# A two-block transformer layer on one core: the residual adds and a LayerNorm's gain moved from GpSimd to VectorE

## What is computed

```python
def rmsnorm(x, g):
    return x * rsqrt(mean(x * x) + EPS) * g
def layer_norm(x, g, b):
    mu, var = mean(x), mean(square(x - mu))
    return (x - mu) * rsqrt(var + LN_EPS) * g + b

# first block
x = x + rmsnorm(merged @ w_out, post_mix_norm)       # "mix residual"
h = rmsnorm(x, pre_mlp_norm)
x = x + rmsnorm(square(relu(h @ w_up)) @ w_down, post_mlp_norm)   # "y residual"
# second block
x = layer_norm(ALPHA * x + hybrid_mixer(x), ln1_g, ln1_b)         # "l1"
x = layer_norm(ALPHA * x + square(relu(x @ w_mlp1)) @ w_mlp2, ln2_g, ln2_b)
```

## Time and profile before

| | |
|---|---|
| median of 3 runs | 2600.52 us (2600.31 to 2602.04) |
| the profiled execution | 2600.69 us, its span 2598.8 us |
| PE | 2554.1 us busy, 98% of the span |
| DVE | 1432.3 us, 55% |
| ACT | 1043.8 us, 40% |
| POOL | 187.0 us, 7% |
| granted TensorE clock | 0.996 of full on average |

### The profile page before, as it was taken

How to read it: one execution, slowest core, us unless ns; L and a number is a source line. 1 busy time by engine, 2 the same in 40 slices (tenths; PEclk the granted TensorE clock), 3 DMA queues, 4 the chain that set the end, 5 groups by cost and what they waited for, 6 DMA issues and landing times.

```text
span 2598.8 us, 30346 instructions
## 1 busy us (share of the span) xinstructions
PE 2554.1 (98%) x12048; PEld 2089.0 (80%) x12048; DVE 1432.3 (55%) x2008; ACT 1043.8 (40%) x1622; POOL 187.0 (7%) x157
## 2 busy tenths in 40 slices
PE   7999999999999999999999999999999999999997
PEld 6777888888887788888888877966788888888886
DVE  4345223334433877666664744255478676576568
ACT  4344222223223554444434542356426444444433
POOL 0000000000020200000000110124011000000001
PEclk9999999999999999999999999999999999999999
DMA  4211211111422427448855441001213364588554
GB/s 163 73 66 65 74 41 41 41 40 57 156 73 87 152 87 240 152 154 309 306 203 194 159 158 47 26 25 34 98 57 130 138 223 152 180 315 315 186 186 146
DMA packets 129677, 347.57 MB, mean 134 GB/s; under 512 B 13152, under 2 KB 13408, under 8 KB 129408
## 3 DMA queue, kind: packets, MB, share of 16 engines
q1 hardware_dynamic: 129536, 345.63, 38.2%
HBM read 256.91 MB, written 85.52 MB: 132 GB/s over the span
## 4 chain that ended last, share of the span: by engine, by line
PE 92%; DVE 3%; issue 2%; ACT 1%; POOL 1%; DMA 1%; SPq 0%; DVEq 0%; POOLq 0%; ACTq 0%
PE bank L633 27%; PE bank L635 27%; PE bank L634 27%; PE bank L1102 2%; PE bank L694 1%; PE bank L1053 1%; POOL accX L2556 1%; PE bank L1079 1%; PE bank L744 1%; PE bank L1080 1%; PE bank L1054 1%; PE bank L811 1%; DVE accX L2505 0%; PE bank L821 0%; PE bank L815 0%
## 5 line engine op out<-in xcount | busy, mean ns | idle before, releaser
L1751 DVE TENSOR_TENSOR wlo<-raw,whi 128x1024 fp32r<-128x1024 f32 x102 | 125.4, 1235 | 276.3 <-ACT whi L1142 275.6
L633 PE MATMUL bank<-hhi,whi 128*128 128x512 f32 x608 | 249.6, 411 | 1.7 <-DVE hlo L1776 1.7
L635 PE MATMUL bank<-hhi,wlo 128*128 128x512 f32 x608 | 239.2, 393 | 0.0
L634 PE MATMUL bank<-hlo,whi 128*128 128x512 f32 x608 | 238.5, 392 | 0.0
L1142 ACT ACTIVATE whi<-raw 128x1024 fp32r<-128x1024 f32 x102 | 106.7, 1054 | 100.6 <-PE bank L635 88.8
L633 PEld LDWEIGHTS bank<-hhi,whi 128*128 128x128 f32 x608 | 115.0, 189 | 29.1 <-issue 6.7
L635 PEld LDWEIGHTS bank<-hhi,wlo 128*128 128x128 f32 x608 | 114.8, 189 | 25.3
L634 PEld LDWEIGHTS bank<-hlo,whi 128*128 128x128 f32 x608 | 115.3, 190 | 22.2
L1447 ACT ACTIVATE r<-r 128x512 f32<-128x512 f32 x78 | 49.1, 629 | 137.6 <-DVE r L2234 100.0
L1102 PE MATMUL bank<-P,va 128*128 128x512 f32 (+1 forms) x192 | 81.5, 509 | 0.0
L2395 DVE TENSOR_REDUCE st<-bank 128x1 f32<-128x128 f32 (+7 forms) x64 | 47.2, 750 | 57.1 <-PE bank L1055 56.9
(11 more groups left out here) (470 smaller groups left out, 7157.3 us busy)
## 6 DMA issues: line engine op xcount, KB each, us to landing
ra<-ud_d SPq DMA_DIRECT2D x112, 512.0 KB, 4.5
raw<-wp_d SPq DMA_DIRECT2D x102, 512.0 KB, 3.6
rbh<-wp_d SPq DMA_DIRECT2D x64, 512.0 KB, 5.8
rawp<-wp_d SPq DMA_DIRECT2D x26, 1024.0 KB, 5.8
ud_d<-us SPq DMA_DIRECT2D x104, 256.0 KB, 5.4
rbw<-wp_d SPq DMA_DIRECT2D x48, 512.0 KB, 3.6
ud_d<-f SPq DMA_DIRECT2D x76, 256.0 KB, 2.0
rbx<-wp_d SPq DMA_DIRECT2D x32, 512.0 KB, 7.5
```

The lines of the kernel that those rows point to most:

```text
L633: e.matmul(P, sh, mh, start=first, stop=False, skip_group_check=more)
L634: e.matmul(P, sh, ml, start=False, stop=False, skip_group_check=more)
L635: return e.matmul(P, sl, mh, start=False, stop=last, skip_group_check=more)
L1751: e.tensor_tensor(out=wlo[n % SLOTS][:, :], in0=raw[n % RAWS][:, :], in1=whi[n % SLOTS][:, :].bitcast(F32), op=ALU.subtract).then_inc(*up( ...
```

## The change

The two residual adds leave GpSimd and stand directly behind VectorE's scaling, in VectorE's queue. In l1, ScalarE's scaling, GpSimd's gain and VectorE's bias (one operation each per tile) become two operations of VectorE: (x - mean) * gain, then times the reciprocal root plus bias. The second one needs ScalarE's root only behind the first. The final LayerNorm (ln2) is not touched.

```diff
--- before.py
+++ after.py
@@ -1732,8 +1732,7 @@
             e.wait_ge(*ok("lx", t))
             e.activation(acc[:, t, :], lx[t % 3][:, :], ACT.Copy, scale=ALPHA).then_inc(*up("za", t))
 
-        ln1 = Pipeline(NT, lambda t: root(st[:, 97 + 4 * t:98 + 4 * t], "l1", t),
-                       l_scale(lambda t: lx[t % 3][:, :], "l1", "l1s", ("att_end",)), nothing, l_transpose, order=(1, 0, 3))
+        ln1 = Pipeline(NT, lambda t: root(st[:, 97 + 4 * t:98 + 4 * t], "l1", t), nothing, nothing, l_transpose, order=(0, 3))
         for g, ks_ in enumerate(CAT_KS):
             run(rows_group(feed, row_product, "w_out_2", ks_, None, (lambda t: ln1.push()) if g == 2 else None))
         def l_root(t):
@@ -2023,6 +2022,9 @@
                 e.wait_ge(*ok("row", 2))
             e.scalar_tensor_tensor(acc[:, t, :], acc[:, t, :], st[:, 4 * t + 1:4 * t + 2], g1[:, :], ALU.mult,
                                    ALU.mult).then_inc(*up("wn", t))
+            e.wait_ge(*ok("wn", t))
+            e.wait_ge(*ok(f"xl{t % 3}", t))
+            e.tensor_tensor(out=acc[:, t, :], in0=acc[:, t, :], in1=xs[t % 3][:, :], op=ALU.add).then_inc(*up("res", t))
 
         def m_scale(t):
             rstd(st[:, 4 * t + 2:4 * t + 3], st[:, 4 * t + 3:4 * t + 4], 1.0 / D, EPS, ("sq2", t), "n2", t)
@@ -2292,6 +2294,9 @@
                 e.wait_ge(*ok("row", 3))
             e.scalar_tensor_tensor(acc2[:, t, :], acc2[:, t, :], st[:, 4 * t + 1:4 * t + 2], g3[:, :], ALU.mult,
                                    ALU.mult).then_inc(*up("yn", t))
+            e.wait_ge(*ok("yn", t))
+            e.wait_ge(*ok(f"x{t}", "a"))
+            e.tensor_tensor(out=acc[:, t, :], in0=acc[:, t, :], in1=acc2[:, t, :], op=ALU.add).then_inc(*up("yr", t))
 
         def y_transposed(t):
             transposed("n3", t, yhi, ylo)
@@ -2465,8 +2470,24 @@
                 e.tensor_tensor(out=dst(t), in0=dst(t), in1=bias[:, :], op=ALU.add).then_inc(*up(done, t))
             return stage
 
-        ln1 = Pipeline(NT, l_stats("l1", lambda t: ("free", "w2", 2, t, 1)), l_mean("l1"), l_bias("l1", lambda t: lx[t % 3][:, :], lb, "lx"),
-                       lambda t: transposed("nz", t, zhi, zlo), order=(1, 2, 0, 3))
+        def l1_normalised(t):
+            m, v = st[:, 96 + 4 * t:97 + 4 * t], st[:, 97 + 4 * t:98 + 4 * t]
+            if t == 0:
+                e.wait_ge(*ok("row", 5))
+            if t < 3:
+                e.wait_ge(*ok("att_end"))
+            else:
+                e.wait_ge(*ok("full", "nz", t - 3, 1))
+                e.wait_ge(*ok("za", t - 3))
+            e.scalar_tensor_tensor(lx[t % 3][:, :], acc[:, t, :], m, lg[:, :], ALU.subtract, ALU.mult).then_inc(*up("l1m", t))
+            e.wait_ge(*ok("rt", "l1", t))
+            e.reciprocal(v, v).then_inc(*up("rstd", "l1", t))
+            e.wait_ge(*ok("rstd", "l1", t))
+            e.wait_ge(*ok("l1m", t))
+            e.scalar_tensor_tensor(lx[t % 3][:, :], lx[t % 3][:, :], v, lb[:, :], ALU.mult, ALU.add).then_inc(*up("lx", t))
+
+        ln1 = Pipeline(NT, l_stats("l1", lambda t: ("free", "w2", 2, t, 1)), l1_normalised, nothing,
+                       lambda t: transposed("nz", t, zhi, zlo), order=(1, 0, 3))
         for g, ks_ in enumerate(CAT_KS):
             run(rows_group(feed, row_product, "w_out_2", ks_, accumulated(("w2", g), acc, ("w2", g - 1)) if g else seeded,
                            (lambda t: ln1.push()) if g == 2 else None))
@@ -2549,24 +2570,6 @@
                 e.tensor_tensor(out=Z[:, m, c], in0=Z[:, m, c], in1=gs[m % 4][:, c], op=ALU.add).then_inc(*up("zz", m, half))
 
 
-
-        def residual(t):
-            e.wait_ge(*ok("wn", t))
-            e.wait_ge(*ok(f"xl{t % 3}", t))
-            e.tensor_tensor(out=acc[:, t, :], in0=acc[:, t, :], in1=xs[t % 3][:, :], op=ALU.add).then_inc(*up("res", t))
-
-        mix = Pipeline(NT, nothing, residual, nothing, nothing, nothing)
-        for t in range(NT):
-            mix.push()
-
-        def y_residual(t):
-            e.wait_ge(*ok("yn", t))
-            e.wait_ge(*ok(f"x{t}", "a"))
-            e.tensor_tensor(out=acc[:, t, :], in0=acc[:, t, :], in1=acc2[:, t, :], op=ALU.add).then_inc(*up("yr", t))
-
-        run(mix.rest())
-        for t in range(NT):
-            y_residual(t)
 
 
         e.wait_ge(*ok("pd", 3))
@@ -2636,16 +2639,6 @@
 
 
 
-        def gain(t):
-            e.wait_ge(*ok("l1s", t))
-            if t == 0:
-                e.wait_ge(*ok("row", 5))
-            e.tensor_tensor(out=lx[t % 3][:, :], in0=lx[t % 3][:, :], in1=lg[:, :], op=ALU.mult).then_inc(*up("l1g", t))
-
-        ln1 = Pipeline(NT, nothing, gain, nothing, nothing)
-        for t in range(NT):
-            ln1.push()
-        run(ln1.rest())
         for t in range(4):
             e.wait_ge(*ok("l2s", t))
             if t == 0:
```

## The result

The changed kernel takes 2607.19 us (median of 12 runs, 2605.38 to 2608.78), the kernel before 2599.78 (12 runs, 2598.44 to 2602.04). The ratio is 1.0027, 95% interval 1.0019 to 1.0034: it is 0.27% slower, 7.4 us by the two medians. 2606.9 was predicted. The profiled execution took 2607.72 us, its span is 2605.7, which is 6.9 us more than before.

A forecast was written before the change was run, and what follows sets the result against it. TensorE, 92% of the chain, was taken to bound the kernel. Delays of 2.1 (mix residual), 0 (y residual) and 4.3 (l1) sum to 6.4 us: span 2598.8 to 2605.2, median 2606.9, range 2602.2 to 2609.5 us.

The forecast's parts named there:

- The sum, 6.4 us: Whole change: delays of 2.1 in the mix residual, 0 in the y residual and 4.3 in l1 add 6.4 us.
- The price of an operation: VectorE's queue: 1.27 us for each of 16 moved adds, and 1.20 us more per l1 tile for 8 tiles.
- half throughput for two float32 sources: l1's two VectorE operations at an estimated 2.4 us each; the whole change would cost some 15 us; chance 0.01.
- Mix residual, +2.1: Mix residual: the weight split TensorE waits for at 888.26 us is done 2.1 us later, delaying TensorE as much.
- The 2.93 us that came back from the lock: Mix residual: without GpSimd's adds, two stretched VectorE operations shorten, 3.03 to 1.28 and 2.41 to 1.23 us.
- Y residual, 0: Y residual: eight moved adds cost TensorE 0 us; the next split is at most 0.7 us late.
- the cover that was named: Y residual: TensorE reaches its piece some 2 us after the split, behind a whole product and two tiles' transpositions.
- l1, +4.3: l1: piece 2's split comes 4.4 us late, costing TensorE 4.3 us, of which 3.1 are spent waiting for `zlo`.
- up to 0.6 for the clock: l1: if the 3.1 us gap lowers TensorE's clock, 1.5 us are lost, mostly hidden: +0.3 to +0.6 us at most.
- The wait of about 1.1 us before piece 2: l1: TensorE would wait about 1.1 us for the split of weight piece 2, after the wait for `zlo`.
- "It moves along and hides nothing": l1: VectorE's 0.75 us idle before the low parts hangs on a chain through ScalarE and gives no slack.
- GpSimd's lock, 0.08: Rival, mix residual: GpSimd's adds block VectorE, so moving them ends the 2.3 us wait at 888.26: 2598.2 us; chance 0.08.

The follow-up runs named there:

- e4: The kernel before without the mix residual's add on any engine (x left out of that sum): 2596.92 us against 2599.96, ratio 0.9987.
- e2: The kernel before with only the y residual's add moved to VectorE: 2600.10 us against 2599.96, ratio 1.0002.
- e3: The kernel before with only l1 changed to two VectorE operations: 2604.92 us against 2599.96, ratio 1.0020.
- e5: The kernel before with l1's two VectorE operations, low part of tile t-3 first and ScalarE's high part before the root: 2601.24 us against 2599.82.
- e11: The kernel before with the final normalisation's root and later stages of tiles 0 to 3 one step later, GpSimd's product kept: 2597.19 us against 2600.05.

## Why the prediction was right, step by step

- **The sum, 6.4 us.** The parts alone measure 6.5 by the medians; the change itself 7.4, with an interval of about 2 us to either side. In the one trace of after, 1.6 us of lower clock in the attention and -0.8 us in the up and down products are scatter and partly cancel. That 2606.9 came within 0.3 us of 2607.19 is in part luck: the kernel before measured 0.7 us less beside the changed one (2599.78) than in the runs that the sum started from (2600.52), which hid most of the 1.0 us by which the change cost more than forecast.
- **The price of an operation.** 1.27 us for an add was right (1.33 to its start less 1.20, plus 1.14). The two operations of l1 took 1.28 us each; half throughput for two float32 sources, to which 0.01 was given, didn't come.
- **Mix residual, +2.1.** Measured +1.8 in the trace and 1.4 in the medians. The tile takes 7.28 us (7.3 said), the wait for tile 3's low part is 1.02 (about 1.1 said). The wait for the split is 0.86 where 1.2 was said: this last number is the term's error of 0.3. The 2.93 us that came back from the lock are confirmed by e4 (3.0).
- **Y residual, 0.** Right: 0.1 in e2 and no wait. The split at about 1517 us had the cover that was named.
- **l1, +4.3, and up to 0.6 for the clock.** Measured +4.6 in the trace, 4.8 and 5.0 in e3. The wait for `zlo` is 3.0 where 3.1 was said. The wait of about 1.1 us before piece 2 did not appear: the split ended at 1973.90 + 1.22 = 1975.12, and TensorE, slowed by the lower clock in between, came to it at 1975.48. The clock took the place of that wait and cost a little more, as the paragraph on the clock had it.
- **"It moves along and hides nothing"**, said of the 0.75 us in front of l1's low parts, is true and was read too briefly. This idle time moved along because it hung on VectorE's own statistics through ScalarE's queue, and e5 shows that it was most of the price: some 3.5 of 5.0 us. For the forecast of this change it made no difference; for judging the idea, it is the main thing.
- **GpSimd's lock, 0.08.** The rival's place and mechanism are real and worth 3.0 us (e4), but the add has to be done by someone, and on a VectorE with 0.49 us of slack in a tile its 1.27 us cost more than the lock did.

## What to carry to other kernels

When work moves between engines, read first where the receiving engine is idle and what that idle time hangs on: a wait that goes through another engine's queue and back to the engine's own work is no slack, it moves along. Such a ring is found by asking, for each idle gap, which instruction stands ahead of the releaser on its engine, and it opens by letting the short dependent instruction come one step later (5.2 us here together with GpSimd's removal, 2.9 alone). What GpSimd's part cost seemed small here (0.3 us) while the ring stood and larger (2.3 us) once it was open, so try an edit that gave nothing once more when the other cause is gone.

## What the runs showed of the hardware

- GpSimd pays for the overlap too, where VectorE's operation was under way first: in e11 GpSimd's product began at 2560.34 us, while VectorE's low part of 2560.04 still ran for 0.92 us, and took 3.19 us in place of 2.41. VectorE's next addition, begun at 2561.17, then took 3.45 us and ended 1.09 us behind the product. A product at 2545.92 that met no such operation at its start took 2.41.
- Behind a wait of 2.97 us the granted clock was 0.66 in the next window of 5 us. Behind one of 2.32 us at 888 us in the kernel before it stayed at 1.00, and behind the same wait in e11 (2.29 us) it fell (0.86 and 0.80 in the windows at 885 and 890 us), although both kernels hold the same instructions up to there. In the attention the clock fell to 0.66 in the changed kernel and in e6 and stayed at 1.00 in the kernel before, with the same waits listed. So the same instructions can get it in one execution and not in another, and it is a part of the scatter between executions.
